# Taking the attention rows' root inside the projection and turning those rows within the first page slots

## The chip, the cores and the metric

The kernel runs on one core of a Trainium2 chip. The metric is the device time of one launch in microseconds (us). The times before come from three runs; the profile is one further execution with the profiler on.

## The reference

One inference step of a two-layer decoder trunk in float32: 512 prompt tokens and 8 samples of 4 new tokens each, whose past of 2048 tokens lies in a paged cache (16 pages of 128 tokens per sample). In each layer one input projection feeds an HGRN2 recurrence (4 heads) and a differential attention (4 heads, two softmax maps each). The part that the change concerns is the prompt's attention output and its per-head norm:

```python
p = jax.nn.softmax(scores)                       # two maps per head
o_d = (p[:, :, 0] - lam * p[:, :, 1]) @ v
od = rms_norm(o_d, diff_norm_w) * (1.0 - lam_init)     # per head of 128
o = concatenate([oh, od], axis=-1)               # oh: the HGRN2 part
h = h + o @ w_o
h = h + hier_moe(rms_norm(h, ffn_norm_w), ...)
```

For the samples the attention runs over the cached pages as well, and the mixture of experts follows in both groups. Outputs are the final rows, the new K and V rows and the HGRN2 states.

## The kernel before

The program is written out by hand, engine by engine, with counting semaphores; each engine runs its list in order. A layer goes through four stages:

1. Norm and projection by tokens (Q, K and V of the attention), with rotary embedding and transposes.
2. Projection by features (`proj_feat`, L659): 32 groups g, each 8 products into bank 6 or 7 that ScalarE evicts (L1226 to L1234: sigmoids and copies). From g = 8 on, the prompt's attention is woven between the groups: scores, `turn_a` (L680), `values` (L689), 16 head tiles in all. The last attention product stands behind g = 26, so g = 27 to 31 are projection alone. VectorE scales each head tile by its row sums (L1757) into `od` and takes its sum of squares (L1760).
3. The page stage: 139 slots s. A slot turns one K page on TensorE (`page_turn`, L700, four transposes into bank 0 or 1), which ScalarE copies to SBUF (L1267); every fourth slot holds the scores of four pages (L711); further places hold the softmax's turns (L733), the values (L750) and one item of the HGRN2 recurrence (`hgrn`). The items of the first slots are four transposes of the value rows each (L770, slots 0, 1, 3, 5). GpSimd takes part in the recurrence's levels (L1895), after three memsets (L1886). The pages come by DMA from SyncE's queue: 8 K buffers, of which K page p is loaded once page p - 8 has been turned (semaphore `kt_ps`), and 5 V buffers of four pages each. SyncE issues in the order four K pages, four V pages.
4. Output projection (L900), norm, router, experts (L950, L974).

Between stages 2 and 3 stands the norm of the prompt's attention rows. ScalarE takes the root of all 16 sums of squares at once after its last eviction (L1255), VectorE takes the reciprocal (L1763) and scales the four row tiles (L1766); TensorE turns each (four transposes, L1011, banks 4 and 5 in turn), and VectorE moves each from the bank into the output projection's operand with its norm weight (L1769). TensorE begins the page stage only behind the fourth of these moves, and so do ScalarE's list (it waits for the fourth turn) and GpSimd's memsets. The semaphores are `od_sq` (sums ready), `od_rt` (root), `od_n` (rows scaled), `od_t` (turned) and `od_ok` (moved).

```python
pe.wait_ge(od_n, n + 1)                 # TensorE, per row tile
if n >= 2:
    pe.wait_ge(od_ok, n - 1)
...
pe.wait_ge(od_ok, PT * (l + 1))         # L1013, ahead of slot 0
act.wait_ge(od_t, PT * (l + 1))         # L1257, ahead of slot 0
pool.wait_ge(od_ok, PT * (l + 1))       # L1918, ahead of the memsets
```

Of the kernel before, what the change touches and what calls it, by code (L numbers as in the profile page):

```python
# [14 lines left out]
ALU = mybir.AluOpType  # L15
ACT = mybir.ActivationFunctionType
# [6 lines left out]
H, DK, HD = 4, 64, 128  # L23
PAST, PAGE = 2048, 128
NPG = PAST // PAGE
P = 128
NS = DB * DT
TOK = S + NS
PT = S // P
# [28 lines left out]
def tok(i):  # L58
    return slice(i * P, i * P + rows(i))
# [109 lines left out]
def build(nc, t_in, t_out):  # L169
# [4 lines left out]
    with ctx:  # L174
# [6 lines left out]
        bank = [ctx.enter_context(nc.psum_tensor(f"bank{i}", [P, 512], F32)) for i in range(8)]  # L181
# [10 lines left out]
        oT = xT  # L192

        def con(name, r=P):
            o, n = at[name]
            return cst[0:r, o:o + n]

        ident, ones, iota = con("ident"), con("ones"), con("iota")
# [35 lines left out]
        od = m_a[:, 3072:5120].rearrange("p (i n) -> p i n", i=PT)  # L234
# [63 lines left out]
        dnw = small("diff_norm_col", (L,))  # L298
# [19 lines left out]
        ssq16 = small("od_ssq", (PT, H))  # L318
        rt16 = small("od_root", (PT, H))
# [56 lines left out]
        od_sq, od_rt, od_n, od_t, od_ok = (sem(x) for x in ("od_sums", "od_roots", "od_normed", "od_t_psum", "od_t_ready"))  # L376
# [36 lines left out]
        def item(s):  # L413

            k = (3 * s + 4) // 5
            return items[k] if 0 <= k < len(items) and 5 * k // 3 == s else (None, 0, 0)
# [163 lines left out]
        def _(pe):  # L580
            mm, tr = nc.tensor.matmul, nc.tensor.transpose
# [101 lines left out]
            def values(l, u):  # L683
# [6 lines left out]
                           start=(j == 0), stop=(j == i))  # L690
                x.then_inc(pa_pv, 1)

            def page_turn(l, s):

                g = l * DB * NPG + s
                pe.wait_ge(kl[s % NK], 16 * (int(s % NK < NT) + l * (DB * NPG // NK) + s // NK + 1))
                if g >= 2:
                    pe.wait_ge(kt_ok, g - 1)
                for h in range(H):
                    x = tr(bank[s % 2][:, h * P:(h + 1) * P], kpage[s % NK][:, h, :], ident)  # L700
                x.then_inc(kt_ps, 1)
# [277 lines left out]
            for l in range(L):  # L979
# [22 lines left out]
                        values(l, v - 3)  # L1002
                pe.wait_ge(fp_ok, 32 * (l + 1))
                pe.wait_ge(pa_ate, 16 * (l + 1))
                for i in range(PT):
                    n = PT * l + i
                    pe.wait_ge(od_n, n + 1)
                    if n >= 2:
                        pe.wait_ge(od_ok, n - 1)
                    for h in range(H):  # L1010
                        x = tr(bank[4 + i % 2][:, h * P:(h + 1) * P], od[:, i, h * P:(h + 1) * P], ident)  # L1011
                    x.then_inc(od_t, 1)
                pe.wait_ge(od_ok, PT * (l + 1))  # L1013
                pe.wait_ge(pa_od, 16 * (l + 1))
                pe.wait_ge(pa_exp, 16 * (l + 1))
                for s in range(SLOTS):
                    if s < DB * NPG:
                        page_turn(l, s)
                    if s % 4 == 0 and 1 <= s // 4 <= NQ:
                        quad_scores(l, s // 4 - 1)  # L1020
                    b, k = s // NPG - 1, s % NPG
                    if k == 2 and b + 1 < DB:
                        new_scores(l, b + 1)
                    if b >= 0:
                        if k in turns(b):
                            turn_p(l, b, turns(b).index(k))
                        if k - 1 in turns(b):
                            quad_values(l, b, turns(b).index(k - 1))
                        if k == turns(b)[4] + 3:
                            turn_o(l, b)  # L1030
                    hgrn(l, item(s))
                pe.wait_ge(so_ok, DB * (l + 1))
                sample_sums(l)
                pe.wait_ge(o_ok, 6 * (l + 1))
# [15 lines left out]
                for j in range(NT):  # L1050

                    later = msk[:, j, :].unsqueeze(1).to_broadcast([P, NT - j, NE])
                    if j == NT - 1:
                        mm(bank[6][:, NE:NT * NE].rearrange("p (i e) -> p i e", e=NE), con("tri"), msk[:, 1:NT, :],
                           start=False, stop=False)
                    x = mm(bank[6][:, (j + 1) * NE:(NT + 1) * NE].rearrange("p (i e) -> p i e", e=NE), ones, later,
                           start=(j == 0), stop=(j == NT - 1))
# [54 lines left out]
        def _(act):  # L1112
# [70 lines left out]
            for l in range(L):  # L1183
# [37 lines left out]
                for g in range(32):  # L1221
                    s, h, half = g // 8, g // 2 % 4, g % 2
                    cols = slice(half * HALF, (half + 1) * HALF)
                    act.wait_ge(fp_ps, 32 * l + g + 1)
                    src = bank[6 + g % 2][:, 0:HALF]
                    if s == 0:  # L1226
                        A(f_h[:, h, cols], src, ACT.Sigmoid)
                        x = A(k_h[:, h, cols], src, ACT.Sigmoid, scale=-1.0)
                    elif s == 1:
                        x = A(i_h[:, h, cols], src, ACT.Copy)  # L1230
                    elif s == 2:
                        x = A(q_h[:, h, cols], src, ACT.Copy, scale=float(HD) ** -0.5)
                    else:
                        x = A(g_h[:, h, cols], src, ACT.Sigmoid)  # L1234
                    x.then_inc(fp_ok, 1)
                    v = g - AT0
                    if 0 <= v < 16:
                        u, U = v, 16 * l + v
                        w = (u // H + 1) * P
                        act.wait_ge(pa_max, U + 1)  # L1240
                        if v >= 2:
                            act.wait_ge(pa_at, U - 1)
                        for c in range(2):
                            x = A(e_p[u % 2][c][:, 0:w], bank[c + 2 * (u % 2)][:, 0:w], ACT.Exp,
                                  bias=mx[:, u % 2, c:c + 1], accum_out=ls[:, u % 2, c:c + 1])
                        x.then_inc(pa_exp, 1)
                    if 2 <= v < 18:
                        u, U = v - 2, 16 * l + v - 2
                        w = (u // H + 1) * P
                        act.wait_ge(pa_at, U + 1)  # L1250
                        if v >= 4:
                            act.wait_ge(pa_pv, U - 1)
                        A(aT[u % 2][:, 0:w], bank[4][:, 0:w], ACT.Copy).then_inc(pa_ate, 1)
                act.wait_ge(od_sq, l + 1)
                A(rt16[:, :, :], ssq16[:, :, :], ACT.Sqrt, bias=con("eps"), scale=1.0 / HD).then_inc(od_rt, 1)  # L1255

                act.wait_ge(od_t, PT * (l + 1))  # L1257
                for s in range(SLOTS):
                    hgrn(l, item(s - 1))
                    if item(s - 3)[0] == "out":  # L1260
# [65 lines left out]
        def _(dve):  # L1326
# [3 lines left out]
            def link(ins, signal=dv):  # L1330

                made[signal.name] = made.get(signal.name, 0) + 1
                ins.then_inc(signal, 1)
                dve.wait_ge(signal, made[signal.name])
# [217 lines left out]
            def o_out(l, b):  # L1552

                B = l * DB + b
                dve.wait_ge(pt_ps, 6 * B + 6)
                link(V.tensor_copy(so.rearrange("p h c t -> p h (c t)"), bank[4][:, 0:P].rearrange("p (h r) -> p h r", h=H)[:, :, 0:2 * DT]))
                link(V.scalar_tensor_tensor(oT[:, H:2 * H, S + b * DT:S + (b + 1) * DT], so[:, :, 1, :], nlam[:, l:l + 1], so[:, :, 0, :],
                                            ALU.mult, ALU.add), so_ok)
# [153 lines left out]
            for l in range(L):  # L1712
# [51 lines left out]
                for i in range(PT):  # L1764
                    o = od[:, i, :].rearrange("p (h n) -> p h n", h=H)
                    link(V.tensor_tensor(o, o, rt16[:, i, :].unsqueeze(2).to_broadcast([P, H, HD]), ALU.mult), od_n)  # L1766
                for i in range(PT):
                    dve.wait_ge(od_t, PT * l + i + 1)
                    link(V.tensor_scalar(oT[:, H:2 * H, tok(i)], bank[4 + i % 2][:, :].rearrange("p (h n) -> p h n", h=H),  # L1769
                                    dnw[:, l:l + 1], None, ALU.mult), od_ok)  # L1770
                queries(l, 0)

                dve.wait_ge(st_v, 16 * NT * (l + 1))
                for s in range(SLOTS):
                    if s % 4 == 0 and 1 <= s // 4 <= NQ:
                        scores_out(l, s // 4 - 1)
                        if s % NPG == 0:
                            max_out(l, s // NPG - 1)
                    b, k = s // NPG - 1, s % NPG
                    if k == 2 and b + 1 < DB:  # L1780
                        new_out(l, b + 1)
                    if k == 8 and b + 2 < DB:
                        queries(l, b + 2)
                    if b >= 0:
                        if k == turns(b)[4] + 2:
                            o_rows(l, b)
                        if k == turns(b)[4] + 3:
                            o_out(l, b)
                    if item(s - 2)[0] == "out":
                        rows_sum(l, item(s - 2)[2])  # L1790
                    if item(s - 3)[0] == "out":
                        rows_normed(l, item(s - 3)[2])
                    if item(s - 2)[0] == "s_norm":
                        sample_rows(l)
                    hgrn(l, item(s))
# [224 lines left out]
```

## Time and profile before

| | us |
|---|---|
| median of three runs | 1936.3 |
| lowest and highest | 1931.23, 1942.03 |
| profiled execution, its own time | 1936.65 |
| its span, first to last instruction | 1935.0 |
| TensorE busy | 1719.6 (89%) |
| VectorE busy | 575.5 (30%) |
| ScalarE busy | 489.1 (25%) |
| GpSimd busy | 170.5 (9%) |
| DMA moved | 465.08 MB, mean 240 GB/s |

Busy shares are averages over stages with different limits; a busy TensorE says nothing of how far it is from its peak. What counts for this change is the stretch between the last projection group and the first page turn, which occurs once in each of the two layers (about 270 to 278 us and 1214 to 1223 us of the span), and the 245 us of pages behind it.

### The profile page before, as it was taken

How to read it: one execution, taken by the hardware profiler on the slowest of the kernel's cores; microseconds unless marked ns; L12 is line 12 of the kernel's file. 1: busy time of each engine (PE TensorE's matmuls, PEld its weight loads, DVE VectorE, ACT ScalarE, POOL GpSimd, SP SyncE). 2: the span in 40 equal slices, each digit the busy share in tenths (PEclk: the TensorE clock that was granted, in tenths of full speed). 3: DMA queues.
4: the chain of work that ended last, by engine and by line, in shares of the span. 5: the costliest groups of instructions: out<-in, count | busy, mean ns of one | idle time of the engine just before them, and what ended most of it. 6: DMA issues, size and time to landing. Idle time of an engine off the chain costs nothing. (4 is left out here: it accounts for less than half of the span.)

```text
span 1935.0 us, 34604 instructions
## 1 busy us (share of the span) xinstructions
PE 1719.6 (89%) x13666; PEld 942.8 (49%) x13666; DVE 575.5 (30%) x1596; ACT 489.1 (25%) x1044; POOL 170.5 (9%) x222
## 2 busy tenths in 40 slices
PE   6999988888896999999599999789888969999991
PEld 3457775664444333333244777566644443333330
DVE  2205626434224211110231253463431251111104
ACT  2013325564411000001111232455542101000012
POOL 1000002201000000000200000130020000000002
PEclk9999989999896999999799999898998969999995
DMA  8422019998744699999842200698898248999994
GB/s 277 156 74 61 6 45 325 299 323 294 258 176 166 228 369 389 401 396 390 291 150 83 95 1 23 208 305 290 291 307 293 77 165 316 399 391 396 383 358 160
DMA packets 215108, 465.08 MB, mean 240 GB/s; under 512 B 23137, under 2 KB 23138, under 8 KB 214946
## 3 DMA queue, kind: packets, MB, share of 16 engines
q1 hardware_dynamic: 197810, 402.40, 58.6%
q0 software_dynamic: 17136, 60.43, 8.2%
q8 instruction: 112, 1.84, 0.4%
q14 instruction: 50, 0.41, 0.1%
HBM read 429.10 MB, written 33.69 MB: 239 GB/s over the span
## 5 line engine op out<-in xcount | busy, mean ns | idle before, releaser
L950 PE MATMUL bank<-wslots,heads 128*32 128x512 f32 (+1 forms) x1568 | 314.6, 607 | 11.4 <-DVE heads L1674 5.5
L659 PE MATMUL bank<-xT,wslots 128*128 128x272 f32 x1024 | 241.8, 393 | 1.5 <-ACT heads L1217 0.8
L659 PEld LDWEIGHTS bank<-xT,wslots 128*128 128x128 f32 x1024 | 191.6, 190 | 40.7 <-issue 3.2
L950 PE MATMUL bank<-hgrn,heads 128*32 128x512 f32 (+1 forms) x736 | 197.2, 593 | 0.0
L700 PE MATMUL bank<-cst,wslots 128*128 128x128 f32 x1024 | 163.2, 287 | 19.1 <-ACT wslots L1267 6.3
L613 PE MATMUL bank<-wslots,xT 128*128 128x512 f32 x384 | 173.2, 605 | 5.2 <-DMA wslots<-in_w_in 3.6
L974 PE MATMUL bank<-wslots,temps 128*32 128x512 f32 (+1 forms) x768 | 169.7, 594 | 0.0
L950 PEld LDWEIGHTS bank<-wslots,heads 128*32 128x32 f32 (+1 forms) x1568 | 91.0, 119 | 159.6 <-issue 152.9
L700 PEld LDWEIGHTS bank<-cst,wslots 128*128 128x128 f32 x1024 | 115.5, 144 | 48.0 <-issue 36.8
L974 PE MATMUL bank<-hgrn,temps 128*64 128x512 f32 (+1 forms) x288 | 127.2, 594 | 1.6 <-DMA wslots<-in_w_down 0.9
L1826 DVE TENSOR_TENSOR temps<-temps,bank 128x512 f32<-128x512 f32 x26 | 17.9, 687 | 366.9 <-PE bank L950 366.9
L900 PE MATMUL bank<-wslots,xT 128*128 128x512 f32 x256 | 116.0, 614 | 3.8 <-DVE xT L1579 3.8
L613 PEld LDWEIGHTS bank<-wslots,xT 128*128 128x128 f32 x384 | 72.5, 194 | 93.5 <-issue 89.7
L1267 ACT ACTIVATE wslots<-bank 128x512 f32<-128x512 f32 x128 | 75.8, 594 | 98.0 <-PE bank L700 89.6
L1267 ACT ACTIVATE heads<-bank 128x512 f32<-128x512 f32 x128 | 74.5, 594 | 100.4 <-PE bank L700 100.2
L950 PE MATMUL bank<-xT,heads 128*32 128x512 f32 (+1 forms) x384 | 86.4, 608 | 3.1 <-DMA wslots<-in_w_up 3.1
L1303 ACT ACTIVATE heads<-bank 128x512 f32<-128x512 f32 x26 | 15.5, 597 | 280.2 <-PE bank L974 280.2
L900 PEld LDWEIGHTS bank<-wslots,xT 128*128 128x128 f32 x256 | 50.0, 198 | 67.1 <-issue 62.9
L950 PEld LDWEIGHTS bank<-hgrn,heads 128*32 128x32 f32 (+1 forms) x736 | 54.7, 117 | 53.5 <-issue 53.5
L1527 DVE TENSOR_SCALAR_CACHE_REDUCE heads<-bank 128x512 f32<-128x512 f32 x64 | 44.3, 692 | 122.5 <-PE bank L711 109.6
L750 PE MATMUL bank<-wslots,heads 128*32 128x128 f32 x2048 | 76.9, 296 | 3.8 <-ACT heads L1282 3.8
L750 PEld LDWEIGHTS bank<-wslots,heads 128*32 128x32 f32 x2048 | 61.3, 119 | 33.6 <-ACT heads L1282 18.0
(306 smaller groups left out, 2041.3 us busy)
## 6 DMA issues: line engine op xcount, KB each, us to landing
wslots<-in_cache_k SPq DMA_DIRECT2D x256, 256.0 KB, 4.5
wslots<-in_cache_v SPq DMA_DIRECT2D x256, 256.0 KB, 4.5
wslots<-in_w_gate SPq DMA_DIRECT2D x22, 2048.0 KB, 15.0
wslots<-in_w_up SPq DMA_DIRECT2D x20, 2048.0 KB, 16.5
wslots<-in_w_down SPq DMA_DIRECT2D x20, 2048.0 KB, 15.5
wslots<-in_w_in SPq DMA_DIRECT2D x14, 2048.0 KB, 9.9
hgrn<-in_w_up SPq DMA_DIRECT2D x12, 2048.0 KB, 16.1
hgrn<-in_w_down SPq DMA_DIRECT2D x10, 2048.0 KB, 13.7
```

The source lines that it names most:

```text
L613: x = mm(bank[2 + m % 2][:, :], xT[:, c, tok(i)], w[:, c, :], start=(c == 0), stop=(c == DC - 1))
L659: x = mm(bank[6 + g % 2][:, 0:HALF], w[:, c, h * P:(h + 1) * P], xT[:, c, half * HALF:(half + 1) * HALF], start=(c == 0), stop=(c == DC - 1))
L700: x = tr(bank[s % 2][:, h * P:(h + 1) * P], kpage[s % NK][:, h, :], ident)
L750: x = mm(bank[5][32 * h:32 * h + 32, 0:HD], ptq[par][:, j, 32 * h:32 * h + 32], vquad[v % NV][:, j, h, :], start=(q == 0 and j == 0), stop ...
L900: x = mm(bank[2 + s][:, :], oT[:, c, tok(i)], w[:, c, :], start=(c == 0), stop=(c == DC - 1))
L950: x = mm(bank[2 + k][a:z, :], xeT[T_ % 2][:, c, a:z], weights((what, l, e), DC)[:, c, :], start=(c == 0), stop=(c == DC - 1))
L974: x = mm(bank[5 + n][a:z, :], hT[T_ % 2][:, c, a:z], weights(("down", l, e), 4)[:, c, n * WB:(n + 1) * WB], start=(c == 0), stop=(c == 3))
L1267: A(ktb[s // 4 % 2][:, s % 4].rearrange("p h n -> p (h n)"), bank[s % 2][:, :], ACT.Copy).then_inc(kt_ok, 1)
L1303: A(yt[b][:, 0:WB], bank[5][:, :], ACT.Copy).then_inc(y_ok, 1)
L1527: tell(V.tensor_scalar(scr[G_ % 6], bank[2][:, :], 1.0, None, ALU.mult, ALU.max, accum_out=mx5[:, g % 4:g % 4 + 1]), sq_ok)
L1826: link(V.tensor_tensor(hgt, silu[T_ % 2], bank[3][:, :], ALU.mult), hg_ok)
```

## The change

The root moves into ScalarE's list behind the eviction of projection group g = 28. The four turns and VectorE's four moves go out of the stretch between the stages into page slots 2 to 5, one each, at the end of the slot on TensorE and ahead of the slot's HGRN2 item on VectorE. TensorE's wait for the fourth move and ScalarE's wait for the fourth turn ahead of slot 0 are gone. GpSimd's wait for the fourth move stays as it is.

```diff
+            def od_turn(l, i):
+
+                n = PT * l + i
+                pe.wait_ge(od_n, n + 1)
+                if n >= 2:
+                    pe.wait_ge(od_ok, n - 1)
+                for h in range(H):
+                    x = tr(bank[4 + i % 2][:, h * P:(h + 1) * P], od[:, i, h * P:(h + 1) * P], ident)
+                x.then_inc(od_t, 1)
...
                 pe.wait_ge(pa_ate, 16 * (l + 1))
-                for i in range(PT):
-                    n = PT * l + i
-                    pe.wait_ge(od_n, n + 1)
-                    if n >= 2:
-                        pe.wait_ge(od_ok, n - 1)
-                    for h in range(H):
-                        x = tr(bank[4 + i % 2][:, h * P:(h + 1) * P], od[:, i, h * P:(h + 1) * P], ident)
-                    x.then_inc(od_t, 1)
-                pe.wait_ge(od_ok, PT * (l + 1))
                 pe.wait_ge(pa_od, 16 * (l + 1))
...
                     hgrn(l, item(s))
+                    if 2 <= s < 2 + PT:
+                        od_turn(l, s - 2)
...
                     x.then_inc(fp_ok, 1)
+                    if g == 28:
+                        act.wait_ge(od_sq, l + 1)
+                        A(rt16[:, :, :], ssq16[:, :, :], ACT.Sqrt, bias=con("eps"), scale=1.0 / HD).then_inc(od_rt, 1)
...
-                act.wait_ge(od_sq, l + 1)
-                A(rt16[:, :, :], ssq16[:, :, :], ACT.Sqrt, bias=con("eps"), scale=1.0 / HD).then_inc(od_rt, 1)
-
-                act.wait_ge(od_t, PT * (l + 1))
...
-                for i in range(PT):
-                    dve.wait_ge(od_t, PT * l + i + 1)
-                    link(V.tensor_scalar(oT[:, H:2 * H, tok(i)], bank[4 + i % 2][:, :].rearrange("p (h n) -> p h n", h=H),
-                                    dnw[:, l:l + 1], None, ALU.mult), od_ok)
                 queries(l, 0)
...
+                    if 2 <= s < 2 + PT:
+                        i = s - 2
+                        dve.wait_ge(od_t, PT * l + i + 1)
+                        link(V.tensor_scalar(oT[:, H:2 * H, tok(i)], bank[4 + i % 2][:, :].rearrange("p (h n) -> p h n", h=H),
+                                             dnw[:, l:l + 1], None, ALU.mult), od_ok)
```

TensorE's order from the last projection group into the first slots, before (L1011 are the rows' turns, L700 the page turns, L770 the value rows' turns, L720 the scores of a sample's own keys):

```order
L659 MATMUL bank7<-xT,wslots 128x272 x8
L1011 MATMUL bank4<-cst,temps 128x128 x4
L1011 MATMUL bank5<-cst,temps 128x128 x4
L1011 MATMUL bank4<-cst,temps 128x128 x4
L1011 MATMUL bank5<-cst,temps 128x128 x4
L700 MATMUL bank0<-cst,wslots 128x128 x4
L770 MATMUL bank6<-cst,hgrn 128x128 x4
L700 MATMUL bank1<-cst,wslots 128x128 x4
L770 MATMUL bank7<-cst,hgrn 128x128 x4
L700 MATMUL bank0<-cst,wslots 128x128 x4
L720 MATMUL bank2<-smalls 32x32 x4
L700 MATMUL bank1<-cst,wslots 128x128 x4
```

And with the change (line numbers of the changed kernel: L700 is now the rows' turn, L710 the page turn, L780 the value rows' turn, L730 the own keys' scores):

```order
L659 MATMUL bank7<-xT,wslots 128x272 x8
L710 MATMUL bank0<-cst,wslots 128x128 x4
L780 MATMUL bank6<-cst,hgrn 128x128 x4
L710 MATMUL bank1<-cst,wslots 128x128 x4
L780 MATMUL bank7<-cst,hgrn 128x128 x4
L710 MATMUL bank0<-cst,wslots 128x128 x4
L730 MATMUL bank2<-smalls 32x32 x4
L700 MATMUL bank4<-cst,temps 128x128 x4
L710 MATMUL bank1<-cst,wslots 128x128 x4
L780 MATMUL bank6<-cst,hgrn 128x128 x4
L700 MATMUL bank5<-cst,temps 128x128 x4
L710 MATMUL bank0<-cst,wslots 128x128 x4
```

The first page turn now follows the projection directly, and the rows' turns stand one to a slot from slot 2 on.

ScalarE's order at the end of the projection, before (L1234 are the sigmoids of groups 24 to 31, L1253 attention copies, L1267 and L1145 the copies of the page stage):

```order
L1234 ACTIVATE hgrn<-bank 128x272
L1253 ACTIVATE temps<-bank 128x512
L1234 ACTIVATE hgrn<-bank 128x272 x6
L1255 ACT_TABLE_LOAD
L1255 ACTIVATE smalls<-smalls,cst 128x16
L1267 ACTIVATE wslots<-bank 128x512
L1145 ACTIVATE hgrn<-bank 128x512
```

And with the change (L1237 the sigmoids, L1259 attention copies, L1241 the root, L1270 and L1148 the copies of the page stage):

```order
L1237 ACTIVATE hgrn<-bank 128x272
L1259 ACTIVATE temps<-bank 128x512
L1237 ACTIVATE hgrn<-bank 128x272 x3
L1241 ACT_TABLE_LOAD
L1241 ACTIVATE smalls<-smalls,cst 128x16
L1237 ACT_TABLE_LOAD
L1237 ACTIVATE hgrn<-bank 128x272 x3
L1270 ACTIVATE wslots<-bank 128x512
L1148 ACTIVATE hgrn<-bank 128x512
```

The root and its table load stand three evictions earlier, and a second table load brings the sigmoids' table back.

## Rows read from the trace of the kernel before

**Rows 1.** Chain that ended last, in time: start us, us, what; its beginning.
```profile
1216.28 0.70 DVE temps L1766
1217.23 1.95 PE bank L1011 x8
...
1222.14 0.76 DVE xT L1769
1222.94 1.12 PE bank L700 x4
```

**Rows 2.** Timeline, layer 1: start us, us, engine, line, operation, [idle before <- releaser].
```profile
1195.34 18.50 PE L659 MATMUL bank<-xT,wslots 128*128 128x272 f32 x80
...
1196.25 0.08 DVE L1760 DVE_READ_ACCUMULATOR2_ANT smalls<- 128x1 f32 x1
...
1202.87 0.40 ACT L1234 ACTIVATE hgrn<-bank 128x272 f32<-128x272 f32 x1 [3.27 <-PE bank L659]
1206.54 0.40 ACT L1234 ACTIVATE hgrn<-bank 128x272 f32<-128x272 f32 x1 [3.27 <-PE bank L659]
...
1213.87 0.40 ACT L1234 ACTIVATE hgrn<-bank 128x272 f32<-128x272 f32 x1 [3.27 <-PE bank L659]
1214.29 1.28 ACT L1255 ACT_TABLE_LOAD   x1
1215.58 0.31 ACT L1255 ACTIVATE smalls<-smalls,cst 128x16 f32<-128x16 f32 x1
1215.99 0.25 DVE L1763 RECIPROCAL smalls<-smalls 128x16 f32<-128x16 f32 x1 [19.66 <-ACT smalls L1255]
1216.28 2.87 DVE L1766 TENSOR_TENSOR temps<-temps,smalls 128x512 f32<-128x512 f32 x4
1217.23 1.94 PE L1011 MATMUL bank<-cst,temps 128*128 128x128 f32 x8 [3.40 <-DVE temps L1766]
...
1222.94 1.12 PE L700 MATMUL bank<-cst,wslots 128*128 128x128 f32 x4 [0.92 <-DVE xT L1769]
```

**Rows 3.** Timeline, layer 0, the same place.
```profile
269.38 0.40 ACT L1234 ACTIVATE hgrn<-bank 128x272 f32<-128x272 f32 x1 [3.27 <-PE bank L659]
...
278.45 1.12 PE L700 MATMUL bank<-cst,wslots 128*128 128x128 f32 x4 [0.92 <-DVE xT L1769]
```

**Rows 4.** Stretches: us; busy of PE, PEld, DVE, ACT, POOL (x); PEclk, DMA share, GB/s.
```profile
1196.00:1214.00 18.00, 17.84 (x78) 14.44 (x76) 0.30 (x2) 1.72 (x5) 0.00 (x0) 1.00 0.00 0
1214.00:1223.00 9.00, 3.94 (x17) 3.12 (x17) 6.11 (x10) 1.86 (x3) 0.05 (x1) 0.62 0.00 0
1223.00:1232.00 9.00, 8.70 (x96) 7.20 (x97) 2.62 (x7) 6.03 (x11) 1.93 (x3) 0.82 0.56 178
1232.00:1242.00 10.00, 8.89 (x222) 6.09 (x221) 7.49 (x16) 5.05 (x9) 1.79 (x2) 1.00 0.95 323
```

**Rows 5.** The same view, layer 0, its first page slots.
```profile
278.40:287.40 9.00, 8.95 (x60) 7.55 (x60) 2.64 (x6) 5.14 (x10) 1.98 (x3) 0.68 0.48 148
```

**Rows 6.** Timeline of TensorE alone, layer 1, slots 1 to 4.
```profile
1224.70 1.06 PE L700 MATMUL bank<-cst,wslots 128*128 128x128 f32 x4
1225.56 0.98 PE L770 MATMUL bank<-cst,hgrn 128*128 128x128 f32 x4
...
1227.60 0.60 PE L770 MATMUL bank<-cst,hgrn 128*128 128x128 f32 x4
1228.04 0.60 PE L700 MATMUL bank<-cst,wslots 128*128 128x128 f32 x4
```

**Rows 7.** One line's instructions: VectorE's moves (L1769), duration ns min/median/max.
```profile
L1769 DVE TENSOR_SCALAR xT<-bank,smalls x8: 751/751/753, 274.7 to 1222.1; 128x512 f32<-128x512 f32 x8
```

**Rows 8.** Timeline, layer 1: SyncE's issues, and the page turn of slot 16.
```profile
1224.25 4.03 SPq L533 DMA_DIRECT2D wslots<-in_cache_k  x4
...
1237.76 2.71 SPq L533 DMA_DIRECT2D wslots<-in_cache_k  x4
...
1242.59 0.66 PE L700 MATMUL bank<-cst,wslots 128*128 128x128 f32 x4 [1.45 <-DMA wslots<-in_cache_k]
```

**Rows 9.** One line's instructions: the sample rows' squares (L1576), behind each layer's page stage.
```profile
L1576 DVE TENSOR_TENSOR temps<-xT x2: 292/292/293, 522.4 to 1471.3; 128x128 f32<-128x128 f32 x2
```

**Rows 10.** Timeline, layer 1: GpSimd.
```profile
1222.95 2.10 POOL L1886 MEMSET temps<- 32x512 f32 x3 [153.66 <-DVE xT L1769]
1239.84 1.08 POOL L1895 TENSOR_TENSOR hgrn<-hgrn 128x272 f32<-128x272 f32 x1 [14.80 <-PE bank L866]
```

## The prediction

> **What bounds the kernel now.** I read the chain of waits first. Followed back from the last instruction it begins at 1216.28 us, with VectorE scaling the attention rows, and goes over the rows' turns and moves into the first page turn and from there, without a hole, to the end [rows 1]. So the small stretch between projection and pages in layer 1 sets the end, and whatever is cut out of it should arrive there, if the pages behind it don't take it back. The timeline shows the stretch piece by piece [rows 2]: the five last projection groups run from 1195.34 for 18.50 us; ScalarE evicts the last at 1213.87 + 0.40 = 1214.27; then come a table load of 1.28, the root 0.31, the reciprocal 0.25, and TensorE begins the first row turn at 1217.23 after 3.40 us of idle time. Turns and moves, two against two banks, last until the first page turn at 1222.94. That is 1222.94 - 1214.27 = 8.7 us in which no page is turned. Layer 0 has the same picture: last eviction at 269.38, first page turn at 278.45 [rows 3]. The reader should also see that the sums of squares were ready at 1196.25 and that ScalarE sat idle 3.27 us ahead of each of its last evictions [rows 2]: the root waits for nothing but its place in ScalarE's list.
>
> **The change, part by part.**
>
> *The root.* It now stands behind the eviction of group 28, which is the one at 1202.87 (31 is the one at 1213.87, 3.67 us apart) [rows 2]. The sums have been there for 7 us, so ScalarE doesn't wait. From 1203.27 on it needs 1.28 + 0.31 + 1.28 (the second load returns to the sigmoids) = 2.87 us, until 1206.14; the next eviction starts at 1206.54 [rows 2]. Cost nothing; its cover is the 3.27 us gap. Were it gone, the cost would be up to 2.87, and TensorE would notice only if the eviction of group 29 came later than the start of group 31 at about 1210.0, over 3 us on. Reciprocal and scaling (0.25 + 2.87 us) follow on VectorE, which has nothing else to do there, and end near 1208.2, some 6 us before the pages begin. So neither root nor scaling is on the path any more.
>
> *The start of the pages.* TensorE now waits for the last eviction only: 1214.27 plus about 0.1 us for a signal (root end 1215.89 to reciprocal 1215.99 [rows 2]), say 1214.4. Gain in layer 1: 1222.94 - 1214.4 = **8.5 us**. In layer 0: 278.45 - 269.9 = **8.55 us** [rows 3].
>
> *The turns in the slots.* Each layer puts four times four transposes into slots 2 to 5. A group of four costs TensorE its pitch: 1228.04 - 1227.60 = 0.44 at full clock and 1225.56 - 1224.70 = 0.86 at half [rows 6]. I take 0.5, since signals stand between: 4 x 0.5 = **2.0 us per layer**; the other end is 4 x 0.86 = 3.4. The best case is 0, since in slot 16 TensorE waits 1.45 us for a K page anyway [rows 8]. The third and fourth turn wait for the first and second move; a move is 0.75 us [rows 7] and has a whole slot, about 1.1 us, so I cost that wait at nothing. VectorE's four moves, 3.0 us, lie beside a VectorE that is busy 2.62 of 9 us there [rows 4]. What stands behind the new waits: on TensorE the next page turn, on VectorE the slot's HGRN2 item, and behind the page turns SyncE's K loads.
>
> *The clock.* TensorE has the full 2.4 GHz until 1214, a mean of 0.62 of it in the gap, 0.82 in the first nine microseconds of pages, then 1.00 again [rows 4]; in layer 0 it is 0.68 in those nine microseconds [rows 5]. The drop follows the 3.40 us of idling, and that idling goes. With levels of 1 and 0.5, a mean of 0.82 is 36% of 9 us at half clock, 3.2 us, and 0.68 is 64%, 5.8 us. Work of a pitch 0.86 done at 0.5 saves 42% of that: **1.4 us in layer 1, 2.4 us in layer 0**. The other end is nothing, if the clock falls in the slots anyway. The Trainium skill ("TensorE: Matmul & The Clock Gate", What's actually happening) states that the throttled clock is the default and that activity releases it; by that rule the clock terms are due in full and the sum is the one below, and if no clock came back 13.05 would be left. The trace agrees as far as it shows the drop right behind an idle stretch.
>
> *Does it carry through the pages?* SyncE's first K load hangs on the first page turn (issued at 1224.25 [rows 8], 0.2 us behind its end), so the page stream starts earlier by the same amount. DMA is at a share of 0.00 from 1196 to 1223, then 0.56, then 0.95 [rows 4]: there is room ahead, and nothing else is in the way. The third batch of K loads is at 1237.76, slot 16 waits for its first page [rows 8]. By the list of issues it should come earlier by 7 to 9 us, because the second batch needs the turns of pages 4 to 7, which the new row turns hold up. GpSimd's memsets now wait for the move in slot 5; before they took 2.10 us and then idled 14.80 until the first level [rows 10], so about 8 us of delay against the page stage still leaves room. Past that the stage's lists are unchanged, and every later load hangs on the stage's own signals.
>
> **The sum.** Layer 1: 8.5 - 2.0 + 1.4 = 7.9. Layer 0: 8.55 - 2.0 + 2.4 = 8.95. Together 16.85. The profiled execution took 1936.65 (span 1935.0 and 1.65 around it), 0.35 above the median of 1936.3. 1936.65 - 16.85 = **1919.8 us**. The bounds of the terms: with free turns 8.5 + 1.4 + 8.55 + 2.4 = 20.85, which is 1915.8; with half clock all along 8.5 + 8.55 - 6.8 = 10.25, which is 1926.4. One measurement of this kernel tells about 0.5% from no change, 9.7 us: faster is below 1926.6, slower above 1946.0.
>
> **The rivals.**
>
> *The turns cost as much inside as outside.* If turn and move ran in lockstep in the slots, with TensorE waiting for VectorE each time, they would last what they last now, 1222.94 - 1217.23 = 5.7 us. Then only the root's wait goes: 8.5 - 5.7 = 2.8 a layer, 5.7 in all, 1931.0. For it speaks that turn and move alternate on two banks; against it that a page turn and value turns now stand between two of them.
>
> *The pages take it back.* The stage runs from 278.45 to 522.4 in layer 0, 243.95 us, and from 1222.94 to 1471.3 in layer 1, 248.4 us [rows 2, 3, 9], with one program. So its own rhythm of loads, clock and waits moves its length by 4.5 us, and a new phase could eat part or, with bad luck in both layers, all: 1936.6. Against it: all its loads start with its first turn.
>
> *GpSimd comes too late, and it gets slower.* The place is the first level of the recurrence. GpSimd's list is in order: a late fourth move delays the memsets, they delay the keys of the levels, TensorE waits for these in order and with it the page turns and K loads. It decides when the memsets, seen from the first page turn, come more than 14.8 us later than now [rows 10]; each microsecond beyond that costs one. To end at 1946.0 both layers would have to lose the 16.85 gained and 9.35 more, 13.1 each: the fourth move would have to come 28 us behind the first page turn, where I expect 9 to 10.
>
> *It doesn't do what it says.* If the sums of squares came after group 28, ScalarE would stand still with the evictions queued behind it. They come 7 us ahead [rows 2], so I give this nothing of its own.
>
> **How the numbers follow.** The forecast with its bounds (1915 to 1926) 0.73; lockstep, 1931.0, 0.14; pages that take most of it back 0.08; GpSimd, or a page rhythm worse than now, slower, 0.04; 0.01 for more than the best sum. The forecast and a part of the second and third, when they lose only a few microseconds, fall below 1926.6: faster 0.77, same 0.19, slower 0.04. The range goes from 1913, the best sum with 3 us of the page stage's own 4.5, to 1931, which takes in lockstep.
>
> **What would show it.** In the changed profile the first page turn follows the last eviction within 0.3 us; the root stands between two sigmoids 3.27 us apart, with a load of 1.28 on either side, and no projection group starts late; the stretch up to the first page turn keeps a clock of 1.00; the four row turns take about 0.5 us of pitch each and show no idle time ahead; the third batch of K loads is 7 to 10 us nearer to the end of the projection; the stage's end, at the sample rows' squares, comes 8 to 9 us nearer to it, in each layer. I am wrong if the row turns show waits for VectorE of a microsecond, or if slot 16 is early and the stage's end is not.

## The result, and the profile after

The changed kernel took **1910.87 us** (median of four runs, 1903.61 to 1915.9), the kernel before in the same comparison 1933.76 (four runs, 1925.35 to 1942.03): a ratio of 0.9881, with a 95% interval of 0.985 to 0.9912. It is faster, as forecast, but by more: 1910.87 lies 2.1 us below the range's lower end of 1913 and 8.9 below the forecast of 1919.8. Its profiled execution took 1914.25, 22.4 less than the 1936.65 of before. Its page, the span and the busy times:

```profile
span 1912.5 us, 34604 instructions
PE 1712.6 (90%) x13666; PEld 938.0 (49%) x13666; DVE 573.6 (30%) x1596; ACT 490.9 (26%) x1046; POOL 170.8 (9%) x222
```

The engines do the same work as before, TensorE in 7.0 us less (1719.6 to 1712.6). The timeline of after in layer 0, from the root to slot 16:

```profile
257.94 0.40 ACT L1237 ACTIVATE hgrn<-bank 128x272 f32<-128x272 f32 x1 [3.27 <-PE bank L659]
258.35 1.28 ACT L1241 ACT_TABLE_LOAD   x1
259.65 0.31 ACT L1241 ACTIVATE smalls<-smalls,cst 128x16 f32<-128x16 f32 x1
259.97 1.28 ACT L1237 ACT_TABLE_LOAD   x1
...
261.60 0.40 ACT L1237 ACTIVATE hgrn<-bank 128x272 f32<-128x272 f32 x1 [0.35 <-PE bank L659]
...
268.94 0.40 ACT L1237 ACTIVATE hgrn<-bank 128x272 f32<-128x272 f32 x1 [3.27 <-PE bank L659]
...
269.39 0.66 PE L710 MATMUL bank<-cst,wslots 128*128 128x128 f32 x4 [0.49 <-ACT hgrn L1237]
...
271.92 0.66 PE L700 MATMUL bank<-cst,temps 128*128 128x128 f32 x4
...
272.41 0.60 PE L710 MATMUL bank<-cst,wslots 128*128 128x128 f32 x4
...
272.69 0.75 DVE L1791 TENSOR_SCALAR xT<-bank,smalls 128x512 f32<-128x512 f32 x1
...
276.61 0.60 PE L700 MATMUL bank<-cst,temps 128*128 128x128 f32 x4
...
277.05 0.60 PE L710 MATMUL bank<-cst,wslots 128*128 128x128 f32 x4
...
278.14 2.10 POOL L1890 MEMSET temps<- 32x512 f32 x3 [153.83 <-DVE xT L1791]
...
286.04 1.07 POOL L1899 TENSOR_TENSOR hgrn<-hgrn 128x272 f32<-128x272 f32 x1 [5.81 <-PE bank L876]
...
287.92 0.66 PE L710 MATMUL bank<-cst,wslots 128*128 128x128 f32 x4
```

Against [rows 2, 3]: the root with its two loads takes the gap between two sigmoids and leaves 0.35 us of it. The first page turn (L710) stands 0.05 us behind the end of the last eviction; before it stood 8.67 behind it. The row turns (L700) have no idle time ahead, and 0.43 to 0.49 us after each the next page turn starts. GpSimd's memsets start 8.75 us behind the first page turn, and its idle time ahead of the first level is 5.81 us (in layer 1 it shrank from 14.80 [rows 10] to 5.80). The stretches of after from the last eviction on, layer 0 and layer 1 (columns as in [rows 4]):

```profile
268.90:277.90 9.00, 8.51 (x111) 7.13 (x110) 3.82 (x8) 5.93 (x12) 0.00 (x0) 1.00 0.71 205
1204.80:1213.80 9.00, 8.58 (x110) 7.20 (x110) 3.89 (x8) 5.97 (x12) 0.00 (x0) 1.00 0.72 221
```

The granted clock is 1.00 where [rows 4, 5] have 0.62 in the gap and then 0.82 and 0.68. At each layer's far end stand the sample rows' squares, in the view of one line's instructions:

```profile
L1579 DVE TENSOR_TENSOR temps<-xT x2: 292/292/292, 511.1 to 1449.9; 128x128 f32<-128x128 f32 x2
```

From the start of the last eviction to them it was 253.0 us in layer 0 and 257.4 in layer 1 [rows 2, 3, 9]; it is 511.1 - 268.94 = 242.2 and 1449.9 - 1204.77 = 245.1. So 10.9 and 12.3 came from these two stretches, where I forecast 8.95 and 7.9; elsewhere the execution lost 0.7 (0.4 gained ahead of layer 0's stretch, 2.2 lost between, 1.1 gained behind). The third batch of K loads, forecast 7 to 10 us nearer to the last eviction, came 11.7 us nearer in layer 0 (25.36 to 13.68) and 9.6 in layer 1 (23.89 to 14.31).

### The profile page after: what moved, and what is told of

It is laid out like the page before. It is cut to its first block and busy times, and to the rows that moved or that the text cites. A ratio compares the mean times of both kernels' runs of the same rounds, so it can differ in the third digit from the quotient of the medians.

```text
span 1912.5 us, 34604 instructions
## 1 busy us (share of the span) xinstructions
PE 1712.6 (90%) x13666; PEld 938.0 (49%) x13666; DVE 573.6 (30%) x1596; ACT 490.9 (26%) x1046; POOL 170.8 (9%) x222
## 5 line engine op out<-in xcount | busy, mean ns | idle before, releaser
L710 PE MATMUL bank<-cst,wslots 128*128 128x128 f32 x1024 | 162.3, 287 | 14.5 <-ACT wslots L1270 6.4
L710 PEld LDWEIGHTS bank<-cst,wslots 128*128 128x128 f32 x1024 | 115.1, 144 | 42.3 <-issue 35.7
L1270 ACT ACTIVATE heads<-bank 128x512 f32<-128x512 f32 x128 | 74.4, 594 | 97.3 <-PE bank L710 96.9
L1270 ACT ACTIVATE wslots<-bank 128x512 f32<-128x512 f32 x128 | 75.8, 594 | 82.5 <-PE bank L710 82.5
```

Source lines behind the costliest of these rows:

```text
L1270: A(ktb[s // 4 % 2][:, s % 4].rearrange("p h n -> p (h n)"), bank[s % 2][:, :], ACT.Copy).then_inc(kt_ok, 1)
```

## The experiments

One ruler serves all of them, worked out from each run's timelines: from the start of the last sigmoid of the projection to the first page turn and to the page turn of slot 16, the first that takes a page of the third K batch. **Gain** is what both layers together are nearer at slot 16 than in the kernel before (30.24 + 28.72).

| run | first page L0 / L1 | slot 16 L0 / L1 | gain | time and before, us | ratio (95%) |
|---|---|---|---|---|---|
| before | 9.07 / 9.07 | 30.24 / 28.72 | 0 | | |
| after | 0.45 / 0.45 | 18.98 / 18.90 | 21.1 | 1910.87, 1933.76 | 0.9881 (0.985 to 0.9912) |
| e1_after_again | 0.45 / 0.45 | 19.37 / 19.38 | 20.2 | 1911.77, 1930.73 | 0.9907 (0.988 to 0.9934) |
| e9_after_third | 0.45 / 0.45 | 19.36 / 19.24 | 20.4 | 1910.87, 1937.43 | 0.9874 (0.985 to 0.9897) |
| e2_before_more_turns | 9.07 / 9.06 | 30.29 / 29.70 | -1.0 | 1936.76, 1930.73 | 1.0023 (1.0005 to 1.0041) |
| e3_after_double_turns | 0.45 / 0.45 | 21.03 / 20.30 | 17.6 | 1915.16, 1930.73 | 0.9922 (0.99 to 0.9944) |
| e4_before_warm | 8.74 / 8.73 | 27.01 / 27.46 | 4.5 | 1924.64, 1930.73 | 0.997 (0.9955 to 0.9986) |
| e5_root_only | 4.45 / 4.45 | 22.61 / 22.66 | 13.7 | 1918.92, 1929.99 | 0.9928 (0.9902 to 0.9955) |
| e6_turns_only | 0.45 / 0.45 | 22.56 / 22.93 | 13.5 | 1919.41, 1929.99 | 0.9935 (0.991 to 0.9959) |
| e7_no_turns | 0.45 / 0.45 | 17.97 / 17.90 | 23.1 | 1908.96, one run | |

### The changed kernel again

No edit; it gives the changed kernel's own scatter beside the other runs.

> The changed kernel as it is, timed again beside the runs that follow. Theory SUM (the terms of the prediction hold: start 8.5 per layer, row turns 2.0 lost per layer, clock 1.4 and 2.4; what was measured beyond is the page stage's own rhythm): about 1917, 17 us below the kernel before, once more runs are in. Theory SLACK (the row turns cost nothing in the slots, since slot 16 waited for a K page that now comes earlier; the rest as in SUM): 21 us below. Theory CLOCK (the clock lost at the first page turns cost more than TensorE's own pitch, since it held up SyncE's loads): 21 to 23 us below. In the profile of all three the stage from the last eviction to the sample rows' squares is 242 to 245 us.

> The changed kernel once more, beside the early page turns of the next run on the same chip. What the runs so far give for the page turn of slot 16 (20 to 21 us nearer to the last evictions than before, both layers together) makes it 0.9895 of the kernel before, give or take 0.003; if it came out at 0.992 or above, slot 16 would not be what the time follows.

Measured: 1911.77 and 1910.87, with gains at slot 16 of 20.2 and 20.4; the mean of the three profiles is 20.6. At slot 16 that is near the 21 of SLACK, and the ratio of 0.9874 lies within what e9_after_third expected; the times alone don't tell the theories apart. The changed kernel's median stays within 0.9 us over three comparisons. The kernel before doesn't: its medians were 1933.76, 1930.73, 1929.99 and 1937.43. The three ratios are gains of 23.0, 18.0 and 24.4 us, on both sides of what separates them.

### What a row turn costs: four groups of transposes added, doubled, left out

Added to the kernel before, in slots 2 to 5, results unused:

```diff
                     hgrn(l, item(s))
+                    if 2 <= s < 2 + PT:
+                        for h in range(H):
+                            tr(bank[4 + s % 2][:, h * P:(h + 1) * P], od[:, s - 2, h * P:(h + 1) * P], ident)
```

> The kernel before, with four row turns more (nothing reads them) in page slots 2 to 5 of each layer; nothing else moves. SUM: 2.0 us per layer at full clock, 3.4 at half: 4 to 7 us slower than before. SLACK: slot 16 waits 1.45 and 1.91 us for its K page in the kernel before, and the turns fill that wait: 0 to 1 us slower, and the wait at slot 16 shrinks by what the turns take. CLOCK: as SUM, 4 to 7 us, since the extra turns fall into the half clock.

Doubled in the changed kernel:

```diff
-                for h in range(H):
-                    x = tr(bank[4 + i % 2][:, h * P:(h + 1) * P], od[:, i, h * P:(h + 1) * P], ident)
+                for h in range(2 * H):
+                    x = tr(bank[4 + i % 2][:, h % H * P:(h % H + 1) * P], od[:, i, h % H * P:(h % H + 1) * P], ident)
```

> The changed kernel with each row turn made twice in its slot (four more groups of four transposes per layer, same result). SUM: 2.0 us per layer, 4 us slower than the changed kernel. SLACK: the changed kernel has 0.51 us of waiting left at slot 16 in layer 1 and none in layer 0, so 3.5 us slower. If it is within 1 us of the changed kernel, TensorE isn't what paces these slots at all, and both are wrong.

Left out of the changed kernel (only the signal is given, so the prompt's attention rows don't reach the output projection; its time as a whole is not to be compared):

```diff
-                for h in range(H):
-                    x = tr(bank[4 + i % 2][:, h * P:(h + 1) * P], od[:, i, h * P:(h + 1) * P], ident)
-                x.then_inc(od_t, 1)
+                pe.sem_inc(od_t, 1)
```

> The changed kernel with the four row turns left out (the moves stay and take what is in the banks), so the prompt's attention part of the output projection's input is not computed; the time behind the page stage is not to be compared, since other experts are chosen. SUM: slot 16's page turn 2.0 us earlier behind the last eviction than in the changed kernel (18.9 to 19.4 us there), about 17. SLACK: slot 16 at the same place within 0.5 us, slot 6 about 1.75 us earlier, and the difference is waiting for the K page ahead of slot 16.

On TensorE the turns cost nearly what I took: to slot 6, behind the last of them, after needs 8.11 - 0.45 = 7.66 us from its first page turn and e7_no_turns 6.37 - 0.45 = 5.92, so four turns are 1.74, and e3_after_double_turns needs 1.75 more. But slot 16 doesn't come later by as much. The chain of waits of after, followed back from slot 16 of layer 1 (start us, us, what):

```profile
1206.75 0.44 PE bank L780 x4
1207.18 0.44 PE bank L710 x4
1207.62 0.20 PE bank L730 x8
1207.82 0.59 PE bank L700 x4
1208.41 0.45 PE bank L710 x4
1208.87 0.05 SPq L533
...
1217.57 0.29 SPq L529
...
1219.08 4.54 DMA wslots<-in_cache_k
...
1223.67 0.66 PE bank L710 x4
```

Only the **first** row turn (1207.82) is on it here, as in e1_after_again. From the page turn behind it, at 1208.87, to the third batch's first K load at 1219.08 the chain is SyncE's own: it issues the last K page of the first batch and four V pages, reads page numbers (L529), issues the next eight and reads page numbers again. The other three row turns run beside that. In e9_after_third, a third execution of the same kernel, all four stand on the chain of layer 1, which goes over to SyncE only at the last K page of the second batch:

```profile
1207.17 0.59 PE bank L700 x4
...
1208.63 0.44 PE bank L700 x4
...
1210.50 0.59 PE bank L700 x4
...
1211.96 0.44 PE bank L700 x4
...
1213.88 0.05 SPq L533
...
1217.98 5.33 DMA wslots<-in_cache_k
```

So the path over the four turns and the path over SyncE's issuing end nearly together, and which is last changes between executions of one kernel. SyncE's issues in after and then in e7_no_turns, layer 1:

```profile
1206.06 3.29 SPq L533 DMA_DIRECT2D wslots<-in_cache_k  x4
1209.45 1.80 SPq L533 DMA_DIRECT2D wslots<-in_cache_v  x4
1212.80 2.82 SPq L533 DMA_DIRECT2D wslots<-in_cache_k  x4
1215.72 1.80 SPq L533 DMA_DIRECT2D wslots<-in_cache_v  x4
1219.08 2.71 SPq L533 DMA_DIRECT2D wslots<-in_cache_k  x4
```

```profile
1205.15 2.86 SPq L533 DMA_DIRECT2D wslots<-in_cache_k  x4
...
1217.84 2.65 SPq L533 DMA_DIRECT2D wslots<-in_cache_k  x4
```

The third batch starts 1219.08 - 1204.77 = 14.31 us behind the last eviction in after and 1217.84 - 1203.86 = 13.98 in e7_no_turns; in layer 0 it is 282.62 - 268.94 = 13.68 and 282.40 - 268.71 = 13.69. The other two profiles of the changed kernel have 13.93 and 13.92 in layer 0, 14.38 and 13.86 in layer 1. So at the issue the four turns cost about 0.2 us per layer, less than the pitch of one. Twice as many are too much for that cover. The chain of e3_after_double_turns in layer 1 doesn't touch SyncE; all four double turns stand on it:

```profile
1213.91 1.02 PE bank L700 x8
...
1215.81 0.87 PE bank L700 x8
...
1218.12 1.02 PE bank L700 x8
...
1220.01 0.87 PE bank L700 x8
```

There slot 16 comes 1.8 and 1.1 us later than in the mean of the changed kernel's three profiles, and the kernel takes 3.4 us more than the changed kernel beside it (1915.16 against 1911.77). In e2_before_more_turns the additional turns mostly fill the wait for a K page that slot 16 had: it falls from 1.91 and 1.45 to 0.39 and 0, and slot 16 moves by 0.05 and 0.98. The whole kernel pays 0.23% for them, 4.4 us (1 to 8): the time is as SUM had it, slot 16 as SLACK had it, and where the rest is lost is not shown. In e7_no_turns slot 16 is 1.3 us earlier per layer (17.97 and 17.90 against a mean of 19.24 and 19.17), between SUM's 2.0 and SLACK's 0.5. Beyond the issue that need not be the turns' price: in layer 1 its K page landed 3.88 us after the issue, in the changed kernel's three profiles 4.54 to 5.33, and no run shows whether that hangs on the turns. The cost of the four turns at slot 16 is thus between 0.2 (the issue) and 1.3 us per layer (all of e7_no_turns); both are below the 2.0 that I took.

### The clock alone: TensorE kept busy in the gap

The kernel before, with transposes of the identity into an idle bank where TensorE waits for the root and for the moves:

```diff
                 for i in range(PT):
                     n = PT * l + i
+                    for _ in range(22 if i == 0 else 5 if i >= 2 else 0):
+                        tr(bank[7][:, 0:P], ident, ident)
                     pe.wait_ge(od_n, n + 1)
...
+                for _ in range(6):
+                    tr(bank[7][:, 0:P], ident, ident)
                 pe.wait_ge(od_ok, PT * (l + 1))
```

> The kernel before, with TensorE kept busy through the gap by transposes of the identity into a bank that nobody reads (22 ahead of the first row turn, 5 ahead of the third and the fourth, 6 ahead of the pages), so that the clock should not fall; root, turns and moves stay where they are. SUM: the clock term alone, 1.4 + 2.4 = 3.8 us faster than before, if the granted clock stays at 1.00 in the first page slots. CLOCK: 7 to 10 us faster. SLACK: 3.8. If the clock stays and the time doesn't move, the clock term was worth nothing.

Its first nine microseconds of pages, layers 0 and 1, columns as in [rows 4]:

```profile
276.90:285.90 9.00, 8.45 (x110) 6.27 (x112) 3.05 (x7) 6.71 (x13) 1.69 (x3) 1.00 0.71 225
1219.20:1228.20 9.00, 8.45 (x110) 6.27 (x112) 3.04 (x7) 6.72 (x13) 1.69 (x3) 1.00 0.77 250
```

The clock is 1.00 instead of 0.68 and 0.82. From the first page turn to slot 16 it is 27.01 - 8.74 = 18.27 and 18.73 us instead of 21.17 and 19.65: 2.9 + 0.9 = **3.8 us**, the sum of my two clock terms (2.4 + 1.4). The split is off because slot 16 also waits for its K page, now longer in layer 1:

```profile
294.87 0.96 PE L700 MATMUL bank<-cst,wslots 128*128 128x128 f32 x4 [1.69 <-DMA wslots<-in_cache_k]
...
1237.62 0.66 PE L700 MATMUL bank<-cst,wslots 128*128 128x128 f32 x4 [2.15 <-DMA wslots<-in_cache_k]
```

Without these waits (1.91 and 1.45 in the kernel before) TensorE saves 2.7 and 1.6. The time falls by 0.3%, 5.8 us (2.7 to 8.7), with not one instruction less; CLOCK, which had 7 to 10, falls. The Trainium skill ("TensorE: Matmul & The Clock Gate", What's actually happening) says that activity releases the throttled clock; the trace agrees, since additional work alone brought 0.68 to 1.00.

### The two halves alone

The root at its new place, turns and moves where they were:

```diff
+                    if g == 28:
+                        act.wait_ge(od_sq, l + 1)
+                        A(rt16[:, :, :], ssq16[:, :, :], ACT.Sqrt, bias=con("eps"), scale=1.0 / HD).then_inc(od_rt, 1)
...
-                act.wait_ge(od_sq, l + 1)
-                A(rt16[:, :, :], ssq16[:, :, :], ACT.Sqrt, bias=con("eps"), scale=1.0 / HD).then_inc(od_rt, 1)
```

> The root moves behind group 28 as in the change; turns and moves stay ahead of the page stage as before. SUM: the first row turn starts 2.85 us earlier per layer, 5.7 us, and since TensorE then idles for half a microsecond ahead of it and not 3.4, part or all of the clock term (3.8) comes with it: 6 to 10 us faster than before. If the clock still falls in the waits between turns and moves (0.92 us each), 6. Slot 16's page turn should stand 2.9 to 5 us nearer to the last eviction than in the kernel before.

Turns and moves in the slots, the root where it was: the reverse of this edit in the changed kernel.

> Turns and moves go into slots 2 to 5 as in the change; the root stays behind the last eviction. The first page turn then comes as early as in the changed kernel, but ScalarE has a table load and the root, 1.6 us, ahead of the first page copy. SUM: the first row turn needs the first scaled tile at about 3.1 us behind the start of the last eviction, where slot 2 has come at about 3.0, so TensorE loses 0 to 0.5 us there and up to 1.6 by the late copies: 0 to 3 us slower than the changed kernel in all, 17 to 20 faster than before. SLACK: slot 16 not later than in the changed kernel by more than 0.5 us per layer. If the root's place were worth its own 2.95 us per layer, it would be 6 us slower than the changed kernel.

Each gives about two thirds: gains of 13.7 and 13.5 at slot 16 (ratios 0.9928 and 0.9935). In e5_root_only I had expected slot 16 to come 2.9 to 5 us nearer per layer; it came 7.6 and 6.1. The row turns follow the last eviction at once, and the first page turn comes at 4.45, behind four turns and moves at full clock (1.00 in both layers), which take 4.00 us where they took 5.82 and 5.71. For e6_turns_only I had expected a smaller loss against the changed kernel: its first page turn stands at 0.45, so I took the root's place for nearly free. The timeline of e6_turns_only, layer 1, and its stretch:

```profile
1212.75 0.40 ACT L1237 ACTIVATE hgrn<-bank 128x272 f32<-128x272 f32 x1 [3.27 <-PE bank L659]
...
1214.46 0.31 ACT L1258 ACTIVATE smalls<-smalls,cst 128x16 f32<-128x16 f32 x1
...
1215.16 2.87 DVE L1767 TENSOR_TENSOR temps<-temps,smalls 128x512 f32<-128x512 f32 x4
...
1218.07 0.35 DVE L1519 COPY smalls<-smalls 64x16 f32<-64x16 f32 x2
...
1218.47 0.27 PE L730 MATMUL bank<-smalls 128*32 128x32 f32 x8 [2.45 <-DVE smalls L1519]
```

```profile
1212.80:1221.80 9.00, 5.92 (x45) 5.43 (x46) 4.49 (x10) 5.56 (x10) 0.00 (x0) 0.85 0.35 95
```

VectorE's list is in order: the queries of sample 0 (L1519) stand behind the scaling of the rows, the scaling behind the root, so TensorE waits 2.45 us at the own keys' scores in slot 2, and in this layer the clock falls to 0.85 (in layer 0 it stays at 1.00). The root's place is worth 7.1 us at slot 16 (20.6 - 13.5) once the turns have moved. The halves don't add up: 13.7 + 13.5 is 6.6 more than 20.6. Both win back clock (3.8 for all of it), and the shorter turns and moves of e5_root_only (3.5 in both layers together) are no longer ahead of the pages in the changed kernel; that would be 7.3, but no run tests this account by itself.

### One step further: eight page turns inside the projection

The first eight pages are in SBUF long before; their turns and copies go behind the last groups, two by two:

```diff
+EARLY = {27: (0, 1), 29: (2, 3), 30: (4, 5), 31: (6, 7)}
...
                     proj_feat(l, g)
+                    if g in EARLY:
+                        pe.wait_ge(pa_exp, 16 * (l + 1))
+                        for s in EARLY[g]:
+                            page_turn(l, s)
...
-                    if s < DB * NPG:
+                    if 8 <= s < DB * NPG:
```

ScalarE's copies move in the same way, behind its eviction of the same group.

> A further step on the changed kernel: the first eight page turns and their copies go into the projection's last groups (two each behind groups 27, 29, 30 and 31), so that the first reload of K pages starts about 16 us before the last eviction; the slots keep everything else. SLACK (behind slot 16 the page stream sets the pace, and SyncE's loads hang on page turns 4 to 8): the third batch of K loads, 13.7 us behind the last eviction in the changed kernel, comes 3 us earlier or more, and the stage ends 3 to 6 us earlier per layer, while the projection is 4 us longer: 0 to 8 us faster than the changed kernel. If TensorE's own work sets the pace from the projection to slot 16, the work has only been moved: the same time within 2 us, slot 16 about 4 us nearer to the last eviction and the projection 4 us longer.

> The early page turns once more. In the profile their page stages were 239.8 and 238.5 us from the last eviction on (changed kernel 242.2 to 246.7) and the projection about 3 us longer per layer. If that is the pages' earlier start and not the stage's own rhythm, it is 2 to 6 us faster than the run before it again; if the work has only been moved, the two are within 2 us.

SyncE's K batches in e8_early_pages, layer 0, whose last eviction is at 271.94:

```profile
255.22 9.05 SPq L534 DMA_DIRECT2D wslots<-in_cache_k  x4
...
267.97 5.38 SPq L534 DMA_DIRECT2D wslots<-in_cache_k  x4
...
279.28 4.00 SPq L534 DMA_DIRECT2D wslots<-in_cache_k  x4
```

The third batch is 7.3 us behind the last eviction instead of 13.7 (in layer 1 9.6 instead of 14.3), and page 16 is turned at 15.0 instead of 19.0, but the eviction itself comes 3 us later, since the projection now holds the turns. The mean from last eviction to the squares is 239.6 us over the four stretches of these two runs and 243.7 over the six of the changed kernel's three. Times: 1906.74 (ratio 0.9883, 0.9856 to 0.991; the changed kernel had 0.9907 in another comparison) and 1909.5 (0.9858, 0.9837 to 0.988, beside 0.9874, 0.985 to 0.9897). The first ratio lies among the changed kernel's three (0.9874 to 0.9907). Where the two ran together it is 1.4 us ahead; the intervals overlap, and e10_early_pages_again had set 2 us as the limit below which the work has only been moved. So it isn't shown to be faster.

## Why the prediction was right, and where it was wrong

- **The root costs nothing: right.** Its 2.87 us lie in the 3.27 us gap; 0.35 is left, no group starts late.
- **The start of the pages: right.** 9.07 - 0.45 = 8.62 per layer, 17.2 in all, where the sum had 17.05.
- **The clock: right**, 3.8 us at slot 16 by e4_before_warm, forecast 3.8, though split 2.9 and 0.9 where I had 2.4 and 1.4.
- **The turns in the slots: the step that failed**, "I take 0.5 ... 2.0 us per layer". The pitch was nearly right (1.74 for four on TensorE), its place on the path wrong: I charged all of it to the path to slot 16. I had named the cover, the K page that slot 16 waits for, but as the best case only; and I argued that the new turns "hold up" the second batch. In layer 1 of before that was so far true, as the chain between first page turn and the third batch ran over TensorE. At full clock TensorE without the turns is ahead of SyncE: e4_before_warm has 1.69 and 2.15 us of waiting for that K page, its layer 1 chain runs over SyncE from 1222.11 on, and from first page turn to slot 16 it takes 18.27 and 18.73 us where after, with row turns in the slots, takes 18.53 and 18.45. The four turns about fill that wait: in the changed kernel's three profiles 0 to 0.98 us of it are left. The term is 0.2 to 1.3 per layer, 0.4 to 2.6 in all by the runs above, instead of 4.0. With 17.2 and 3.8, the three profiles' mean gain of 20.6 leaves about half a microsecond. Where in that span it lies stays open.
- **It carries through the pages: right.** The gain at slot 16 forecasts the whole kernel: 20.6 against 18.0 to 24.4 measured, 17.6 against 15.1 (e3_after_double_turns), 13.7 against 13.9, 13.5 against 12.5, 4.5 against 5.8. The exception is e2_before_more_turns, where 1.0 is lost at slot 16 and 4.4 (1 to 8) in all. So *the pages take it back* falls. Behind slot 16 a stage takes 222 to 229 us in all of these kernels; with one to three profiles of each I see no order in that scatter.
- **Lockstep: fell.** No row turn waits; before a move VectorE idles at most 0.56 us, and only GpSimd's memsets wait for one.
- **GpSimd too late: fell**, with 5.81 us of slack left and the memsets at 8.75, forecast 9 to 10.
- **The range's lower end.** The miss of 8.9 us splits into 4.2 of terms (21.1 - 16.85), 1.3 in the rest of the profiled execution (22.4 - 21.1) and 3.4 by which the changed kernel's profiled execution (1914.25) lies above its median. The bounds of the terms gave 1915.8 at best, and I put 3 us below that for the page stage. What I left out is that before's own runs spread over 1931 to 1942, so a sum against one execution of 1936.65 may be off by several microseconds whatever the change. The mis-sized turns alone don't explain the miss: 1936.65 - 20.6 is 1916.1, inside the range. The four medians of before average 1933.0; from there 20.6 leads to 1912.4, near the 1910.87 to 1911.77 measured. A lower end 5 us further down (1936.3 - 1931.23), at 1908, would have taken that in.

## What to carry to other kernels

Place a moved piece of work on the chain as it will be after the change: once the stall is gone, another queue (here SyncE's issuing) may be the late one, and work beside it is cheap until it outgrows that cover, as the doubled turns did. Read that chain in more than one execution: two of one kernel's profiles had one row turn on it, the third all four. A wait moved off one engine can come back through the in-order list of another (VectorE's queries behind the scaling), so the two halves of such a change may need each other. Where a gap on TensorE can't be removed, look at the granted clock behind it; keeping the engine busy in the gap gave 0.3% here.

## What was not expected of the hardware

- A DMA issuing queue can carry the critical chain by itself: 10.2 us of after's chain (1208.87 to 1219.08) are SyncE issuing 13 page loads and reading page numbers twice; a batch of four V pages takes 1.80 us to issue, and the next K batch starts 1.55 us behind it.
- The second table load of the root's detour starts as soon as the root ends and ahead of the sigmoid's wait for its group (259.97, against the sigmoid at 261.60), so it is hidden in that wait.
- The kernel before had medians of 1929.99 to 1937.43 in four comparisons, the changed kernel of 1910.87 to 1911.77 in three. Why the one moves more than the other stays open.
